# Two of the four turns of the first side group as seven block products, run side by side

## The chip, the cores and the metric

The kernel is one program on one core of a Trainium2 chip. Five engines of that core run their own instruction queues and meet only at semaphores: TensorE (PE: matrix products, weights loaded by PEld), VectorE (DVE), ScalarE (ACT), GpSimd (POOL) and SyncE (SP, which issues transfers). The metric is device time in microseconds (us) from start to end of one execution, as the median of several runs.

## The reference, cut to what matters

Two transformer-like blocks follow each other on one sequence of 256 tokens with 2048 features. All weights and results are fp32.

```
x = x + (y * silu(gate)) @ w_out                    # first block: gated MLP mixer, 3 * 4096 columns in
z = rmsnorm_2(x, g) @ w_in                          # second block, one wide product, 10256 columns
fq, fk, fv, mq, mk, mv, ...  = slices of z          # two kinds of attention heads
x = x + (g_a * (a_out @ w_proj_a) + g_m * (m_out @ w_proj_m)) @ w_out
x = x + (silu(conv(h2 @ w_up)[gate]) * conv(h2 @ w_up)[val]) @ w_down
```

Nearly all arithmetic is in such products of 256 tokens with weight matrices that are read once. The change lies in `z = ... @ w_in`: in the first 512 columns of `fq` and the first 512 of `fk`, which the kernel computes together.

## The kernel before

**A weight chunk.** The weights are one stream of chunks of 512 KB: 128 partitions by 1024 numbers, which are two blocks of 128 rows by 512 columns. Every chunk goes through the same four stations. SP loads it into one of four `raw` buffers. ACT copies it into `w_hi` in a reduced fp32 format (line 1339). DVE subtracts, `w_lo = raw - w_hi` (line 1834). PE then makes three products of each block with the activations, which are split in the same way: high with high, high with low, low with high. `w_hi` and `w_lo` have four slots each, so ACT may begin an item when PE is done with the item four places earlier.

**Items and turns.** The work is a list of items in an order that tables write out by hand. A chunk item is one chunk for both halves of the tokens: 12 matmuls of 128x512. A group is two sets of 512 columns; over 2048 rows it has four turns of 512 rows, and a turn is four chunk items (C0 to C3, C0 and C1 for the first column set, C2 and C3 for the second). A turn can also be taken as seven products of sums of blocks (the scheme of Strassen and Winograd), each an item of 6 matmuls: products 1, 5, 7, 6, 3, 2 and 4. Four blocks B11, B12, B21 and B22 of the weights are then combined: product 1 takes B11, product 5 the sum of B11 and B12, and so on. The sums of weight blocks are made by DVE (lines 1839 and 1853) and by two adding transfers that POOL issues (line 2572); the sums of the activations' rows are made once per turn ahead of time, by five DVE instructions, one ACT copy and one DVE subtraction.

**The side group.** The phase `vv` (two groups) is followed by the phase `side` (six groups). Until now the first side group has turn 0 by products and turns 1, 2 and 3 by chunks: 12 chunk items and 7 products, in the order `MID_PAIRED`. Products 1, 5, 7 and 6 go into two banks of their own (1 and 7 into one, 5 and 6 into the other); ACT copies 1, 5 and 7 out before the bank is used again, and DVE combines them (`mid_own_products`). Products 2, 3 and 4 add straight into the group's result banks.

**What else hangs on the items.** Numbered slots (`SLOTS`) tie small tasks to items; an item without a slot carries none. In slot 0, ACT and DVE split the gate weights `gw_raw` into `gw_both` (lines 1668 and 1883). In slot 2, after its item, PE makes the gate logits from `gw_both` (`gate_logits`, line 1086). The results of the first half of the group are normalised per head: ACT squares them at slot 14, DVE reduces and POOL takes a power, DVE scales them at slot 16 (`q_scaled`), and PE transposes them after slot 18 (line 833). All engines work through their queues in program order, so an instruction that waits holds everything behind it.

**SP's loads.** SP issues the ring's loads as lows are made, and the first two weight blocks of a turn by products (`mq_block`, line 681) at the items that `BLOCKS_AT` names, in the same queue.

Of the kernel before, what the change touches and what calls it, by code (L numbers as in the profile page):

```python
# [58 lines left out]
for _name, _w in (("a_norm", KD), ("norm1", KD), ("norm2", KD), ("b_s", GROUPS),  # L59
# [40 lines left out]

SUM_TURNS = {"v": (3, 2), "out1": (4, 5), "vv": (0,), "down": (0, 1, 2, 6), "gm0": (3, 2), "out2": (1,)}


SUMS_AT = {"v": (4, 8), "out1": (2, 6), "vv": (-7,), "down": (3, 7, 11, 64), "gm0": (-8, -5), "out2": (-7,)}

# [11 lines left out]

MID_TURN = 0
MID_PAIRED = ((1, "C0"), (1, "C1"), (1, "C2"), (1, "C3"), (2, "C0"), 1, 5, (2, "C1"), (2, "C2"), (2, "C3"), 7, 6,
# [9 lines left out]
NO_SLOT = {MID_PAIRED: (5, 10, 14), MID_SINGLE: (8, 14, 16), MID_EARLY: (8, 14, 16), MID_PLAIN: ()}  # L129
SLOTS = {}  # L130
# [19 lines left out]
for _name, _counts in PHASES:  # L150
    FIRST_ITEM[_name] = len(ITEMS)
    if _name == "ug":
        for _g in range(GROUPS):
            for _step in UG_ORDER if _g else UG_FIRST:
                if isinstance(_step, int):
                    ITEMS.append(Item("ug", _g, _step, UG_TURN, None, None))
                else:
                    _turn, _k = _step[0], int(_step[1][1])
                    ITEMS.append(Item("ug", _g, 0, _turn, _k // 2, 2 * _turn + _k % 2))
        continue  # L160
    if _name in MID_ORDER:
# [25 lines left out]
def in_ring(item):  # L187
# [31 lines left out]
             FIRST_ITEM["side"] - 3: ("side", B12), FIRST_ITEM["side"] - 2: ("side", B11),  # L219
             FIRST_ITEM["side"] + 64: ("side", B11, 4), FIRST_ITEM["side"] + 65: ("side", B12, 4),  # L220
             FIRST_ITEM["ug"] - 6: ("ug", B11), FIRST_ITEM["ug"] - 5: ("ug", B12),
# [38 lines left out]
def quads_ahead(phase):  # L260

    return sum(FIRST_ITEM[name] < FIRST_ITEM[phase] for name, _, _ in QUADS)


def next_in_place(item):

    if item.phase == "side" and item.group not in (0, 1):
        return None
    return (UG_NEXT_IN_PLACE if item.phase in SPREAD else NEXT_IN_PLACE).get(item.product)

# [7 lines left out]
def loads_of_block(q, b):  # L278

    return sum(phase not in SPREAD or b in (B11, B12) for phase, _, _ in QUADS[:q + 1])  # L280


def spread_quads(q):

    return sum(phase in SPREAD for phase, _, _ in QUADS[:q + 1])


def mid_quads(phase, g):

    return sum(name in MID_ORDER and (FIRST_ITEM[name], group) < (FIRST_ITEM[phase], g) for name, group, _ in QUADS)  # L290

# [14 lines left out]
def sums_made(q, p):  # L306


    ahead = sum(1 if phase == "ug" else 2 if phase in MID_ORDER else 4 for phase, _, _ in QUADS[:q])
    return ahead + ({5: 1, 4: 2} if QUADS[q][0] in MID_ORDER else {5: 1, 7: 2, 6: 3, 4: 4})[p]  # L310


def buffer_of(q, b):

    return b if b == B21 or QUADS[q][0] in SPREAD else (b + q - quads_ahead(QUADS[q][0])) % 3

# [42 lines left out]
def group_of(phase, g):  # L359
# [5 lines left out]
    else:  # L365
# [4 lines left out]
FIRST_APART_HEADS = tuple(max(0, (SLOTS["side"][_n] - HEAD_AT) // 4)  # L370
                          for _n in (MID_SINGLE.index(1) + len(MID_PAIRED), MID_SINGLE.index(1) + len(MID_PAIRED + MID_SINGLE)))

# [23 lines left out]
def build(nc, x, x_tokens, stream, w_s, params, gain_rows, final_rows, gate_w, identity, consts, out):  # L396
# [121 lines left out]
    GA_PLACE = (2, 3, 0, 1)  # L518
    mid_sums = Sums(sb, "mid", [("y", 48 * kib)], [("y", 52 * kib)], ("y", 0), ("y", 4 * kib))
    mid_wide = {}  # L520
    for name, phase, groups, blocks, halves in (
            ("mv", "vv", (0, 1), (8, 12), (40, 44)), ("mq", "side", (0,), (8, 12), (40, 44)),
            ("mk", "side", (1, 2), (56, 60), (40, 44)), ("ma", "side", (4,), (8, 12), (56, 60))):
        made = Mid(sb, name, blocks, halves, mid_sums)
        mid_wide.update({(phase, g): made for g in groups})
# [138 lines left out]
    with block:  # L664

        @block.sync
        def _(sp):
# [10 lines left out]
            def load_block(q, b):  # L678

                phase, g, _ = QUADS[q]  # L680
                sp.dma_start(wide(phase, g).blocks[buffer_of(q, b)][:], stream[block_row(q, b)]).then_inc(block_full[b], 16)


            for n, item in enumerate(ITEMS):
# [17 lines left out]
                if n in BLOCKS_AT:  # L702
# [21 lines left out]
                    load_block(QUADS.index((phase, of[0], MID_TURN)) if of else quads_ahead(phase), b)  # L724
                if n in GAIN_AT:
# [14 lines left out]
        def _(pe):  # L740
# [575 lines left out]
        def _(act):  # L1316
# [3 lines left out]
            def high_of_chunk(n):  # L1320

                item = ITEMS[n]
                if not in_ring(item):
                    b, q = PRODUCT_OF[item.product], quad_of(item)
                    of = wide(item.phase, item.group).blocks[buffer_of(q, b)]
                    if item.product in (1, 3, 2):
                        act.wait_ge(block_full[b], 16 * loads_of_block(q, b))
                    elif item.phase in SPREAD and item.product != 5 and not (item.phase in MID_ORDER and item.product == 4):
                        act.wait_ge(sem[f"block_added{item.product}"], 16 * spread_quads(q))
                    else:  # L1330
                        act.wait_ge(sem["block_sums"], sums_made(q, item.product))
# [257 lines left out]
            def mid_copies(at_item):  # L1589
# [232 lines left out]
        def _(dve):  # L1822
# [18 lines left out]
            def block_sums(n):  # L1841

                item, before = ITEMS[n], ITEMS[n - 1]
                if item.product == 1:
                    q = quad_of(item)
                    dve.wait_ge(block_full[B11], 16 * loads_of_block(q, B11))
                    dve.wait_ge(block_full[B12], 16 * loads_of_block(q, B12))
                    dve.wait_ge(lo_ready, n + 1)
                    block_sum(item, B11, B12, B11)
                elif item.phase in MID_ORDER and item.product == 2:  # L1850
                    dve.wait_ge(lo_ready, n + 1)
                    to = wide(item.phase, item.group).blocks[B11]
                    v.tensor_tensor(to[:], to[:], raw[:, CHUNK_COUNT[n] % RING, :], ALU.add).then_inc(sem["block_sums"], 1)
# [698 lines left out]
        def _(pool):  # L2552
# [6 lines left out]
            def add_block(n):  # L2559
# [10 lines left out]
                else:  # L2570
                    pool.wait_ge(lo_ready, n + 1)
                p.dma_start(wide(item.phase, item.group).blocks[to][:], stream[block_row(q, b)], accum_op=ALU.add).then_inc(
                    sem[f"block_added{product}"], 16)

# [96 lines left out]
```

## Time and profile before

| | |
|---|---|
| median of 3 runs | 2072.61 us (2071.7 to 2073.15) |
| the profiled execution, its own time | 2071.87 us |
| its span, first to last instruction | 2069.9 us |
| PE busy | 2065.7 us |
| DVE busy | 1647.2 us |
| ACT busy | 1167.7 us |

The profile is of one execution; the 1.97 us by which its own time exceeds its span lie before the first and after the last instruction. Times inside it are counted from the span's start. A busy PE is not PE at its peak: matmuls overlap, so a group's busy time per matmul is longer than the distance from one start to the next.

### The profile page before, as it was taken

The page shows a single profiled execution, that of the slowest core. Times are in us where ns is not written, and L with a number is a line of the kernel's source. Part 1 is how long each engine was busy: PE and PEld are TensorE (multiplying, and loading weights), DVE is VectorE, ACT ScalarE, POOL GpSimd, SP SyncE. Part 2 cuts the span into 40 slices and gives each one's busy share as a digit, 9 for nine tenths or more (in the row PEclk, how much of TensorE's full clock was granted, in tenths as well). Part 3 has the DMA queues.
Part 4 walks back from the last instruction along what each step waited for, and adds up shares of the span by engine and source line. Part 5 has one row for each costly group of instructions (what it writes and reads, how often), then busy time and mean ns, then how long its engine had stood idle before and what let it go on. Part 6 is the DMA issues. An engine that isn't in the chain of part 4 may idle for free.

```text
span 2069.9 us, 25490 instructions
## 1 busy us (share of the span) xinstructions
PE 2065.7 (100%) x9902; PEld 1734.3 (84%) x9902; DVE 1647.2 (80%) x1853; ACT 1167.7 (56%) x1392; POOL 50.1 (2%) x53
## 2 busy tenths in 40 slices
PE   9999999999999999999999999999999999999999
PEld 8888888888888887888888888888888888888887
DVE  7888888887888876886788778867777777789986
ACT  6766555555556555665555555555555555555553
POOL 0000000000000000110000000000000000000000
PEclk9999999999999999999999999999999999999999
DMA  9657777777684767655465656455555565556653
GB/s 345 209 198 221 224 233 226 210 245 220 247 262 153 219 206 215 206 158 192 136 232 182 206 185 219 158 187 179 190 187 191 192 196 181 193 182 236 226 202 131
DMA packets 117719, 423.28 MB, mean 204 GB/s; under 512 B 13152, under 2 KB 13920, under 8 KB 117344
## 3 DMA queue, kind: packets, MB, share of 16 engines
q1 hardware_dynamic: 109440, 394.66, 56.0%
q0 software_dynamic: 5184, 18.88, 5.2%
q10 hardware_dynamic: 2976, 8.14, 1.1%
q8 instruction: 78, 1.28, 0.2%
q14 instruction: 41, 0.34, 0.1%
HBM read 419.52 MB, written 2.10 MB: 204 GB/s over the span
## 4 chain that ended last, share of the span: by engine, by line
PE 99%; DMA 0%; ACT 0%; DVE 0%; SPq 0%; issue 0%; DVEq 0%; ACTq 0%
PE g L922 51%; PE xs L968 9%; PE xs L784 8%; PE g L784 8%; PE g L972 7%; PE g L755 4%; PE xs L790 4%; PE g L790 4%; PE xs L833 1%; PE xs L1009 1%; PE xs L1142 0%; DMA raw<-in_stream 0%; PE xs L1139 0%; PE xs L1156 0%; PE xs L1086 0%; PE xs L1169 0%
## 5 line engine op out<-in xcount | busy, mean ns | idle before, releaser
L1834 DVE TENSOR_TENSOR w_lo<-raw,w_hi 128x1024 fp32r<-128x1024 f32 x627 | 760.2, 1222 | 303.9 <-ACT w_hi L1339 296.3
L1339 ACT ACTIVATE w_hi<-raw 128x1024 fp32r<-128x1024 f32 x627 | 657.5, 1057 | 519.6 <-PE g L922 228.1
L922 PE MATMUL g<-w_hi,in_both 128*128 128x512 f32 x1104 | 350.6, 390 | 0.0
L922 PE MATMUL g<-w_hi,mid_both 128*128 128x512 f32 x960 | 310.7, 393 | 0.0
L922 PEld LDWEIGHTS g<-w_hi,in_both 128*128 128x128 f32 x1104 | 207.2, 188 | 42.9
L922 PE MATMUL g<-w_lo,in_both 128*128 128x512 f32 x552 | 214.7, 389 | 0.0
L922 PEld LDWEIGHTS g<-w_hi,mid_both 128*128 128x128 f32 x960 | 180.3, 188 | 37.3
L922 PE MATMUL g<-w_lo,mid_both 128*128 128x512 f32 x480 | 186.9, 389 | 0.0
L784 PE MATMUL g<-mlp_both,w_hi 128*128 128x512 f32 x704 | 167.0, 391 | 0.0
L784 PE MATMUL xs<-mlp_both,w_hi 128*128 128x512 f32 x704 | 165.6, 390 | 0.0
L784 PEld LDWEIGHTS xs<-mlp_both,w_hi 128*128 128x128 f32 x704 | 130.7, 188 | 26.2
L784 PEld LDWEIGHTS g<-mlp_both,w_hi 128*128 128x128 f32 x704 | 130.3, 188 | 26.0
L922 PEld LDWEIGHTS g<-w_lo,in_both 128*128 128x128 f32 x552 | 103.6, 188 | 21.3
L922 PEld LDWEIGHTS g<-w_lo,mid_both 128*128 128x128 f32 x480 | 90.3, 188 | 18.0
L922 PE MATMUL g<-w_hi,f_hi 128*128 128x512 f32 x240 | 93.5, 390 | 0.0
L922 PE MATMUL g<-w_hi,f_lo 128*128 128x512 f32 x240 | 93.4, 389 | 0.0
L922 PE MATMUL g<-w_lo,f_hi 128*128 128x512 f32 x240 | 93.4, 389 | 0.0
L790 PEld LDWEIGHTS g<-mlp_both,w_lo 128*128 128x128 f32 x704 | 88.3, 191 | 2.3
L790 PE MATMUL g<-mlp_both,w_lo 128*128 128x256 f32 x704 | 89.0, 283 | 0.0
L790 PEld LDWEIGHTS xs<-mlp_both,w_lo 128*128 128x128 f32 x704 | 87.4, 192 | 1.7
L790 PE MATMUL xs<-mlp_both,w_lo 128*128 128x256 f32 x704 | 87.9, 283 | 0.0
L1339 ACT ACTIVATE w_hi<-d_block 128x1024 fp32r<-128x1024 f32 x49 | 52.0, 1062 | 56.5 <-PE g L922 40.3
(521 smaller groups left out, 3395.7 us busy)
## 6 DMA issues: line engine op xcount, KB each, us to landing
raw<-in_stream SPq DMA_DIRECT2D x627, 512.0 KB, 4.2
d_block<-in_stream SPq DMA_DIRECT2D x28, 512.0 KB, 4.4
o_block<-in_stream SPq DMA_DIRECT2D x24, 512.0 KB, 4.8
v_block<-in_stream SPq DMA_DIRECT2D x20, 512.0 KB, 4.4
gm_block<-in_stream SPq DMA_DIRECT2D x16, 512.0 KB, 5.7
ge_block<-in_stream POOLq DMA_DIRECT2D x15, 512.0 KB, 6.0
ge_block<-in_stream SPq DMA_DIRECT2D x10, 512.0 KB, 4.9
gl_block<-in_stream POOLq DMA_DIRECT2D x6, 512.0 KB, 5.4
```

The lines of the kernel that those rows point to most:

```text
L755: ins = mm(G[buf][:, t, :], a[:, kt, at_t], w[:, slot, j * COLS:(j + 1) * COLS], start=(kt == 0 and n == 0), stop=(last and j == ROWS_PER_ ...
L784: return mm(UP[buf][:, b, :, :], w_hi[:, slot, j * COLS + b * P:j * COLS + (b + 1) * P], a_both[:, :, kt, :], start=(kt == 0), stop=last a ...
L790: ins = mm(UP[buf][:, b, 0, :], w_lo[:, slot, j * COLS + b * P:j * COLS + (b + 1) * P], a_both[:, 0, kt, :], start=False, stop=(last and j ...
L833: ins = turn(TR[:, b, t * P:(t + 1) * P], of[:, t, b * P:(b + 1) * P], ident[:])
L922: ins = mm(GG[:, bank, :], a[:, kt, t * P:(t + 1) * P], w[:, slot, half_chunk(j)], start=n == 0 and opens(item, bank), stop=ended and n == ...
L968: ins = mm(XS[:, own[p], :], a, w[:, slot, half_chunk(j)], start=first and opens_own(item), stop=last and j == 1 and n == 2, skip_group_ch ...
L972: ins = mm(GG[:, RESULT_OF[p], :], a, w[:, slot, half_chunk(j)], start=first and opens(item, RESULT_OF[p]), stop=False, skip_group_check=True)
L1009: ins = mm(SV[:, t, :], w[:, t, :], a[:, t, :], start=(n == 0), stop=(n == 2))
L1339: activation(w_hi[:, n % RING, :], of[:], ACT.Copy).then_inc(hi_ready, 1)
L1834: v.tensor_tensor(w_lo[:, n % RING, :], of, w_hi[:, n % RING, :].bitcast(F32), ALU.subtract).then_inc(lo_ready, 1)
```

## The change

The first side group now takes two turns by products, turn 0 and turn 1, and turns 2 and 3 by chunks. A table `MID_DOUBLE` writes the new order out: 8 chunk items and 14 products (a minus marks turn 1's), side by side, so that both turns' products of one number add into the same bank and are copied out once. The second turn's blocks have places of their own (`mq_block` 2 and 3), two more loads at the group's start and semaphores of their own; its row sums are made in the second `vv` group. The slots of the 22 items are again 16.

```
-SUM_TURNS = {... "vv": (0,), ...}
+SUM_TURNS = {... "vv": (0, 1), ...}
-SUMS_AT = {... "vv": (-7,), ...}
+SUMS_AT = {... "vv": (-7, 24), ...}
+MID_DOUBLE = ((2, "C0"), (2, "C1"), 1, -1, (3, "C0"), 5, -5, (3, "C1"), (2, "C2"), 7, -7, (2, "C3"), 6, -6, 2, -2, 4,
+              (3, "C2"), -4, 3, -3, (3, "C3"))
-             "side": (MID_PAIRED, MID_SINGLE, MID_SINGLE, MID_PLAIN, MID_EARLY, MID_PLAIN)}
+             "side": (MID_DOUBLE, MID_SINGLE, MID_SINGLE, MID_PLAIN, MID_EARLY, MID_PLAIN)}
+NO_SLOT = {MID_DOUBLE: (3, 6, 10, 13, 15, 19), ...}
+             FIRST_ITEM["side"] - 1: ("side", B12, 0, MID_SECOND), FIRST_ITEM["side"]: ("side", B11, 0, MID_SECOND),
-            ... ("mq", "side", (0,), (8, 12), (40, 44)),
+            ... ("mq", "side", (0,), (8, 12, 56, 60), (40, 44)),
+    def block_in(q, b):
+        return (second_full[b], 16) if second(q) else (block_full[b], 16 * loads_of_block(q, b))
...
+                if item.product == 5 and item.turn == MID_SECOND:
+                    pe.wait_ge(sem["sums_lo_ready"], sums_ahead("vv") + 2)
...
-                if p not in (1, 5, 7):
+                if p not in (1, 5, 7) or item.turn != last_by_products(phase, g):
                     return
...
+                sums_high("vv", n)
...
+                sums_low("vv", n)
+                sums_of_rows("vv", n, norm_mid.hi, norm_mid.lo)
```

On SP, where the side group's first blocks are loaded, the queue was this (`raw` are ring loads, `mq_block_113` and `mq_block_112` are B12 and B11 of turn 0):

```order
L681 DMA mq_block_113<-in_stream 128x1024
L696 DMA raw<-in_stream 128x1024 [waits lo_ready]
L681 DMA mq_block_112<-in_stream 128x1024
L696 DMA raw<-in_stream 128x1024 [waits lo_ready] x9
L681 DMA mk_block_117<-in_stream 128x1024 [waits lo_ready]
```

and is now (`mq_block_115` and `_114` are turn 0's B12 and B11, `_117` and `_116` those of turn 1):

```order
L708 DMA mq_block_115<-in_stream 128x1024
L723 DMA raw<-in_stream 128x1024 [waits lo_ready]
L708 DMA mq_block_114<-in_stream 128x1024
L723 DMA raw<-in_stream 128x1024 [waits lo_ready]
L708 DMA mq_block_117<-in_stream 128x1024
L723 DMA raw<-in_stream 128x1024 [waits lo_ready]
L708 DMA mq_block_116<-in_stream 128x1024
L723 DMA raw<-in_stream 128x1024 [waits lo_ready] x4
L708 DMA mk_block_121<-in_stream 128x1024 [waits lo_ready]
```

Two loads of 512 KB now stand between ring loads that followed each other before.

On DVE, from the last `vv` group's results (`mv_half`) to the gate weights (`gw_both`), this stood before:

```order
L2195 TENSOR_TENSOR mv_half_110<-g,mv_half_110 128x1024 [waits own_read,mm_done]
L1834 TENSOR_TENSOR w_lo<-raw,w_hi 128x1024 [waits hi_ready] x2
L2195 TENSOR_TENSOR mv_half_111<-g,mv_half_111 128x1024 [waits own_read,mm_done]
L1834 TENSOR_TENSOR w_lo<-raw,w_hi 128x1024 [waits hi_ready] x2
L2307 TENSOR_TENSOR fold<-ident 32x16
L1883 TENSOR_TENSOR gw_both<-gw_raw,gw_both 128x16x16 [waits gw_hi_ready]
```

and now:

```order
L1864 TENSOR_TENSOR w_lo<-raw,w_hi 128x1024 [waits hi_ready]
L1864 TENSOR_TENSOR w_lo<-mq_block_114,w_hi 128x1024 [waits hi_ready]
L1869 TENSOR_TENSOR mq_block_114<-mq_block_115,mq_block_114 128x1024 [waits lo_ready,block_full1,block_full0]
L2225 TENSOR_TENSOR mv_half_113<-g,mv_half_113 128x1024 [waits own_read,mm_done]
L1864 TENSOR_TENSOR w_lo<-mq_block_116,w_hi 128x1024 [waits hi_ready]
L1869 TENSOR_TENSOR mq_block_116<-mq_block_117,mq_block_116 128x1024 [waits lo_ready,second_full1,second_full0]
L1864 TENSOR_TENSOR w_lo<-raw,w_hi 128x1024 [waits hi_ready]
L2339 TENSOR_TENSOR fold<-ident 32x16
L1913 TENSOR_TENSOR gw_both<-gw_raw,gw_both 128x16x16 [waits gw_hi_ready]
```

Both block sums and the low of turn 1's product 1 now stand ahead of the gate weights on DVE.

On DVE, near the end of the group, from the small gate sums (`gr`, `b_cum`) to the first steps of combining the own products (`mq_half`), this stood before:

```order
L2323 TENSOR_SCALAR gr<-xs 128x2x8 [waits cum_ready]
L2324 COPY b_cum<-xs 128x8
L2325 COPY gr<-gz 128x2x4
L2326 TENSOR_TENSOR gr<-gz,xs 128x2x4
L1834 TENSOR_TENSOR w_lo<-raw,w_hi 128x1024 [waits hi_ready]
L1853 TENSOR_TENSOR mq_block_112<-mq_block_112,raw 128x1024 [waits lo_ready]
L1834 TENSOR_TENSOR w_lo<-raw,w_hi 128x1024 [waits hi_ready]
L2177 TENSOR_TENSOR mq_half_115<-mq_half_114,xs 128x512 [waits mm_done,p1_ready]
L1834 TENSOR_TENSOR w_lo<-mq_block_112,w_hi 128x1024 [waits hi_ready,dve_step]
```

and now:

```order
L1883 TENSOR_TENSOR mq_block_114<-mq_block_114,raw 128x1024 [waits lo_ready]
L1864 TENSOR_TENSOR w_lo<-raw,w_hi 128x1024 [waits hi_ready]
L2355 TENSOR_SCALAR gr<-xs 128x2x8 [waits cum_ready]
L2356 COPY b_cum<-xs 128x8
L2357 COPY gr<-gz 128x2x4
L2358 TENSOR_TENSOR gr<-gz,xs 128x2x4
L1883 TENSOR_TENSOR mq_block_116<-mq_block_116,raw 128x1024 [waits lo_ready]
L1864 TENSOR_TENSOR w_lo<-mq_block_114,w_hi 128x1024 [waits hi_ready]
L1864 TENSOR_TENSOR w_lo<-raw,w_hi 128x1024 [waits hi_ready]
L2207 TENSOR_TENSOR mq_half_119<-mq_half_118,xs 128x512 [waits mm_done,p1_ready]
L1864 TENSOR_TENSOR w_lo<-mq_block_116,w_hi 128x1024 [waits hi_ready,dve_step]
```

A second block sum stands in this stretch now, and the first one has moved ahead of the gate sums.

## Rows read from the trace of the kernel before

**Rows 1.** The page, parts 1 and 4: busy times, and the chain by engine.

```profile
PE 2065.7 (100%) x9902; PEld 1734.3 (84%) x9902; DVE 1647.2 (80%) x1853; ACT 1167.7 (56%) x1392; POOL 50.1 (2%) x53
...
PE 99%; DMA 0%; ACT 0%; DVE 0%; SPq 0%; issue 0%; DVEq 0%; ACTq 0%
```

**Rows 2.** Timeline, PE: start, us, engine, line, operation, idle before and its releaser.

```profile
777.49 0.39 PE L972 MATMUL g<-w_hi,mid_both 128*128 128x512 f32 x1
...
778.85 0.39 PE L972 MATMUL g<-w_hi,mid_sums_hi 128*128 128x512 f32 x1
...
794.95 0.39 PE L922 MATMUL g<-w_hi,mid_both 128*128 128x512 f32 x1
...
795.17 3.86 PE L1086 MATMUL xs<-mid_both,gw_both 128*32 128x512 f32 x16
```

**Rows 3.** Timeline, SP's issues at the group's start.

```profile
780.54 0.43 SPq L681 DMA_DIRECT2D mq_block<-in_stream  x1
782.63 29.86 SPq L696 DMA_DIRECT2D raw<-in_stream  x9
```

**Rows 4.** Tile mq_block on SP, two loads: time from issue to landing.

```profile
DMA to landing us min/median/max: 5.2/5.2/5.3
```

**Rows 5.** Windows: stretch and length, busy us of five engines, PEclk, DMA share, GB/s.

```profile
6.00:9.00 3.00, 3.00 (x15) 2.62 (x15) 2.94 (x6) 2.65 (x6) 0.00 (x0) 1.00 1.02 412
...
780.00:790.00 10.00, 10.00 (x46) 8.29 (x45) 9.49 (x10) 5.65 (x8) 0.00 (x0) 1.00 0.91 309
```

**Rows 6.** Timeline, DVE and ACT round the gate weights.

```profile
781.39 2.35 DVE L1834 TENSOR_TENSOR w_lo<-raw,w_hi 128x1024 fp32r<-128x1024 f32 x2
...
792.62 0.43 DVE L1883 TENSOR_TENSOR gw_both<-gw_raw,gw_both 128x256 fp32r<-128x256 f32 x1 [0.23 <-ACT gw_both L1668]
...
792.71 1.06 ACT L1339 ACTIVATE w_hi<-mq_block 128x1024 fp32r<-128x1024 f32 x1
...
793.80 1.23 DVE L1834 TENSOR_TENSOR w_lo<-mq_block,w_hi 128x1024 fp32r<-128x1024 f32 x1 [0.76 <-ACT w_hi L1339]
...
795.16 1.23 DVE L1839 TENSOR_TENSOR mq_block<-mq_block,mq_block 128x1024 f32<-128x1024 f32 x1
```

**Rows 7.** Timeline, DVE, ACT and PE at the end of the group and after it.

```profile
825.43 0.68 DVE L2180 TENSOR_TENSOR mq_half<-mq_half,mq_half 128x512 f32<-128x512 f32 x1
826.83 1.23 DVE L1834 TENSOR_TENSOR w_lo<-raw,w_hi 128x1024 fp32r<-128x1024 f32 x1 [0.72 <-ACT w_hi L1339]
...
829.30 2.35 DVE L1834 TENSOR_TENSOR w_lo<-raw,w_hi 128x1024 fp32r<-128x1024 f32 x2
...
840.91 1.23 DVE L2283 TENSOR_TENSOR mq_half<-mq_half,q_factor 128x1024 f32<-128x1024 f32 x1
```

**Rows 8.** Timeline, PE after the group: a small transposition, and those that want q_scaled.

```profile
828.13 0.38 PE L1110 MATMUL xs<-ident,gr 128*32 128x128 f32 x2
...
843.34 1.03 PE L833 MATMUL xs<-ident,mq_half 128*128 128x128 f32 x8
```

**Rows 9.** Timeline, ACT at an item's end: the wait that ended on PE.

```profile
779.11 1.06 ACT L1339 ACTIVATE w_hi<-raw 128x1024 fp32r<-128x1024 f32 x1 [0.30 <-PE g L972]
```

**Rows 10.** Timeline, DVE: row sums of a turn as they stand before.

```profile
687.07 1.22 DVE L1928 TENSOR_TENSOR mid_rows<-mid_both 128x1024 f32<-128x1024 f32 x1
...
689.57 0.42 DVE L1934 TENSOR_TENSOR mid_sums<-mid_rows,mid_sums 128x256 f32<-128x256 f32 x1
```

**Rows 11.** Timeline, DVE in the second vv group, where row sums are added.

```profile
763.40 1.22 DVE L1834 TENSOR_TENSOR w_lo<-mv_block,w_hi 128x1024 fp32r<-128x1024 f32 x1
765.25 1.23 DVE L1834 TENSOR_TENSOR w_lo<-mv_block,w_hi 128x1024 fp32r<-128x1024 f32 x1 [0.62 <-ACT w_hi L1339]
...
768.03 1.23 DVE L1834 TENSOR_TENSOR w_lo<-raw,w_hi 128x1024 fp32r<-128x1024 f32 x1 [0.37 <-ACT w_hi L1339]
```

**Rows 12.** Lines, DVE, 787 to 845 us: line, shape, count, busy and mean, idle before.

```profile
L1834 DVE TENSOR_TENSOR w_lo<-raw,w_hi 128x1024 fp32r<-128x1024 f32 x18 | 21.8, 1221 | 13.7 <-ACT w_hi L1339 13.7
```

**Rows 13.** Tile mq_block on POOL, two adding transfers: time from issue to landing.

```profile
DMA to landing us min/median/max: 5.4/5.6/5.8
```

More of the change, by code:

```diff
@@ L115 @@
 UG_HALF_ENDS = (16, 18)
-MID_TURN = 0
+MID_TURN, MID_SECOND = 0, 1
 MID_PAIRED = ((1, "C0"), (1, "C1"), (1, "C2"), (1, "C3"), (2, "C0"), 1, 5, (2, "C1"), (2, "C2"), (2, "C3"), 7, 6,
@@ L164 @@
                 if isinstance(_step, int):
-                    ITEMS.append(Item(_name, _g, _step, MID_TURN, None, None))
+                    ITEMS.append(Item(_name, _g, abs(_step), MID_TURN if _step > 0 else MID_SECOND, None, None))
                 else:
@@ L219 @@
              FIRST_ITEM["side"] - 3: ("side", B12), FIRST_ITEM["side"] - 2: ("side", B11),
-             FIRST_ITEM["side"] + 64: ("side", B11, 4), FIRST_ITEM["side"] + 65: ("side", B12, 4),
+             FIRST_ITEM["side"] + 67: ("side", B11, 4), FIRST_ITEM["side"] + 68: ("side", B12, 4),
+             FIRST_ITEM["side"] - 1: ("side", B12, 0, MID_SECOND), FIRST_ITEM["side"]: ("side", B11, 0, MID_SECOND),
              FIRST_ITEM["ug"] - 6: ("ug", B11), FIRST_ITEM["ug"] - 5: ("ug", B12),
@@ L268, in next_in_place @@
         return None
+    if item.phase == "side" and item.turn != last_by_products("side", item.group):
+        return None
     return (UG_NEXT_IN_PLACE if item.phase in SPREAD else NEXT_IN_PLACE).get(item.product)
@@ L278, in loads_of_block, with second @@
 def loads_of_block(q, b):
-    return sum(phase not in SPREAD or b in (B11, B12) for phase, _, _ in QUADS[:q + 1])
+    return sum(not second(k) and (QUADS[k][0] not in SPREAD or b in (B11, B12)) for k in range(q + 1))
+def second(q):
+    return QUADS[q][0] in MID_ORDER and QUADS[q][2] == MID_SECOND
 def spread_quads(q):
-    return sum(phase in SPREAD for phase, _, _ in QUADS[:q + 1])
+    return sum(QUADS[k][0] in SPREAD and not second(k) for k in range(q + 1))
 def mid_quads(phase, g):
-    return sum(name in MID_ORDER and (FIRST_ITEM[name], group) < (FIRST_ITEM[phase], g) for name, group, _ in QUADS)
+    return sum(name in MID_ORDER and (FIRST_ITEM[name], group) < (FIRST_ITEM[phase], g) for name, group in GROUPS_BY_PRODUCTS)
 def item_at_slot(phase, c):
@@ L309, in sums_made @@
     ahead = sum(1 if phase == "ug" else 2 if phase in MID_ORDER else 4 for phase, _, _ in QUADS[:q])
+    if second(q):
+        return ahead + {5: 0, 4: 2}[p]
+    if q + 1 < len(QUADS) and second(q + 1):
+        return ahead + {5: 1, 4: 3}[p]
     return ahead + ({5: 1, 4: 2} if QUADS[q][0] in MID_ORDER else {5: 1, 7: 2, 6: 3, 4: 4})[p]
 def buffer_of(q, b):
+    if second(q):
+        return b + 2
     return b if b == B21 or QUADS[q][0] in SPREAD else (b + q - quads_ahead(QUADS[q][0])) % 3
@@ L370 @@
 FIRST_APART_HEADS = tuple(max(0, (SLOTS["side"][_n] - HEAD_AT) // 4)
-                          for _n in (MID_SINGLE.index(1) + len(MID_PAIRED), MID_SINGLE.index(1) + len(MID_PAIRED + MID_SINGLE)))
+                          for _n in (MID_SINGLE.index(1) + len(MID_DOUBLE), MID_SINGLE.index(1) + len(MID_DOUBLE + MID_SINGLE)))
 def heads_before(c):
@@ L518, in build @@
     GA_PLACE = (2, 3, 0, 1)
-    mid_sums = Sums(sb, "mid", [("y", 48 * kib)], [("y", 52 * kib)], ("y", 0), ("y", 4 * kib))
+    mid_sums = Sums(sb, "mid", [("y", 48 * kib), ("y", 16 * kib)], [("y", 52 * kib), ("y", 20 * kib)], ("y", 0), ("y", 4 * kib))
     mid_wide = {}
     for name, phase, groups, blocks, halves in (
-            ("mv", "vv", (0, 1), (8, 12), (40, 44)), ("mq", "side", (0,), (8, 12), (40, 44)),
+            ("mv", "vv", (0, 1), (8, 12), (40, 44)), ("mq", "side", (0,), (8, 12, 56, 60), (40, 44)),
             ("mk", "side", (1, 2), (56, 60), (40, 44)), ("ma", "side", (4,), (8, 12), (56, 60))):
@@ L645, in build, with block_added @@
     block_full = [sem[f"block_full{b}"] for b in range(4)]
+    second_full = [sem[f"second_full{b}"] for b in (B11, B12)]
+    def block_in(q, b):
+        return (second_full[b], 16) if second(q) else (block_full[b], 16 * loads_of_block(q, b))
+    def block_added(q, product):
+        if second(q):
+            return sem[f"second_added{product}"], 16
+        return sem[f"block_added{product}"], 16 * spread_quads(q)
     hi_ready, lo_ready, mm_done = sem["hi_ready"], sem["lo_ready"], sem["mm_done"]
@@ L680, in load_block @@
                 phase, g, _ = QUADS[q]
-                sp.dma_start(wide(phase, g).blocks[buffer_of(q, b)][:], stream[block_row(q, b)]).then_inc(block_full[b], 16)
+                sp.dma_start(wide(phase, g).blocks[buffer_of(q, b)][:], stream[block_row(q, b)]).then_inc(block_in(q, b)[0], 16)
             for n, item in enumerate(ITEMS):
@@ L723, in _ @@
                         sp.wait_ge(sem["y_ready"], GROUPS)
-                    load_block(QUADS.index((phase, of[0], MID_TURN)) if of else quads_ahead(phase), b)
+                    load_block(QUADS.index((phase, of[0], of[1] if len(of) > 1 else MID_TURN)) if of else quads_ahead(phase), b)
                 if n in GAIN_AT:
@@ L1326, in high_of_chunk @@
                     if item.product in (1, 3, 2):
-                        act.wait_ge(block_full[b], 16 * loads_of_block(q, b))
+                        act.wait_ge(*block_in(q, b))
                     elif item.phase in SPREAD and item.product != 5 and not (item.phase in MID_ORDER and item.product == 4):
-                        act.wait_ge(sem[f"block_added{item.product}"], 16 * spread_quads(q))
+                        act.wait_ge(*block_added(q, item.product))
                     else:
@@ L1845, in block_sums @@
                     q = quad_of(item)
-                    dve.wait_ge(block_full[B11], 16 * loads_of_block(q, B11))
-                    dve.wait_ge(block_full[B12], 16 * loads_of_block(q, B12))
+                    dve.wait_ge(*block_in(q, B11))
+                    dve.wait_ge(*block_in(q, B12))
                     dve.wait_ge(lo_ready, n + 1)
@@ L1851, in block_sums @@
                     dve.wait_ge(lo_ready, n + 1)
-                    to = wide(item.phase, item.group).blocks[B11]
+                    to = wide(item.phase, item.group).blocks[buffer_of(quad_of(item), B11)]
                     v.tensor_tensor(to[:], to[:], raw[:, CHUNK_COUNT[n] % RING, :], ALU.add).then_inc(sem["block_sums"], 1)
@@ L2571, in add_block @@
                     pool.wait_ge(lo_ready, n + 1)
-                p.dma_start(wide(item.phase, item.group).blocks[to][:], stream[block_row(q, b)], accum_op=ALU.add).then_inc(
-                    sem[f"block_added{product}"], 16)
+                p.dma_start(wide(item.phase, item.group).blocks[buffer_of(q, to)][:], stream[block_row(q, b)], accum_op=ALU.add).then_inc(
+                    block_added(q, product)[0], 16)
             pool.wait_ge(sem["minus_half_ready"], 1)
```

8 lines of the change are left out of this document (4 added, 4 removed).

## The prediction

> **What bounds the kernel now.** I read the page first. PE is busy for 2065.7 of the 2069.9 us, and the chain that ended last runs on PE for 99% of the span [rows 1]. So only two things move the time: how much PE has to issue, and whether PE is made to wait where it does not wait now. Next I read the timeline of the first side group on PE. Six matmuls of 128x512, which are one product, start 1.36 us apart from the next six (777.49 to 778.85), so a matmul costs PE 0.227 us and a chunk item of 12 costs 2.72 us [rows 2]. The 0.39 us that stands beside each matmul overlaps with its neighbours and is not the price. Then I read the timeline of DVE and ACT there, because both must feed each item, and SP's issues and landings, because two loads are added.
>
> **The change part by part.**
>
> *Matmuls.* Turn 1 took four chunk items, 48 matmuls, and takes seven products, 42. Six matmuls fewer at 0.227 us give **-1.36 us**. This lies on the path as a whole, since PE is the path.
>
> *Row sums in the second vv group.* They add five DVE instructions, 687.07 to 689.99 in the place where they stand now, 2.9 us [rows 10], one ACT copy like the 1.06 us ones, and one DVE low of 1.2 us. They fall behind the low that ends at 763.4. The four DVE instructions that follow move by up to 2.9 us, of which the waits before them take back 0.62 and 0.37 us [rows 11], so the low at 768.03 ends near 771.2 instead of 769.3. Its item is the first chunk after product 6, and PE comes to it at 772.0: product 2 starts at 777.49 [rows 2], and two chunks of 2.72 us stand ahead of it. The cover is 0.8 us. I cost this at nothing. Were the cover gone it would cost as much as it falls short, at most 1 us, since the DVE has waits of its own again afterwards.
>
> *The gate weights: a new wait on PE.* Here I expect most of the price. Products 1 of both turns now come third and fourth in the group, where they came sixth. In the clock of the old trace PE ends the third item before the gate logits at 795.17 [rows 2]; with a product (1.36) in place of a chunk (2.72) it is ready for the gate logits at 793.81. They need `gw_both`, which DVE makes behind the low of turn 1's product 1, its block sum and the low of a chunk. That low waits for ACT, which waits for B11 of turn 1 to land, with everything else of ACT queued behind.
> - Its issue: SP issues the ring load behind the low at 781.39, at 782.63, then B12; the second low of that pair ends at 781.39 + 2.35 = 783.74, and then come another ring load and B11, at about 784.1 by my estimate [rows 3, 6].
> - Its landing: turn 0's B11 is issued at 780.54 and lands 5.2 us later, at 785.7 [rows 3, 4]. Behind it stand a ring load, B12, a ring load and B11 of turn 1, four times 0.524 MB. The fastest stretch shown moves 412 GB/s, 1.27 us each; 780 to 790 moves 309 GB/s, 1.70 us each, with a DMA share of 0.91 [rows 5]. At full share that stretch gives 340 GB/s, 1.54 us. I take 1.35 us, nearer to the faster, since the transfers then stand in line without a break: 785.7 + 5.4 = 791.1. Early end: B11 takes the same 5.2 us from its own issue, 789.3. Late end: 4 times 1.70, 792.5.
> - From there: ACT's high and the step to DVE's low take 1.09 us (792.71 to 793.80), low to block sum 1.36 us (793.80 to 795.16), the block sum and the chunk's low 1.14 each before the next may start (of two lows in 2.35 us, the first holds the second for 1.12), `fold` about 0.1 by my estimate, being far smaller than `gw_both`, and `gw_both` itself 0.43 [rows 6]. Together 5.3 us after the landing: 796.4.
> - PE is ready at 793.8, so it waits **2.6 us**; at the early end 0.8, at the late end 4.0. If the load lands before 788.5, not at all.
>
> A rule speaks here too. By the Trainium skill (DMA: Bandwidth & Descriptors, Specifications) a core's share of HBM is about 358 GB/s; that makes 1.46 us for each load as an estimate, a landing at 791.5 and a wait of 3.0 us in place of 2.6, and the sum +1.9 in place of +1.5. The trace goes above this figure for a while (412 GB/s), so the measurement decides, and the rule is no end of my range.
>
> *Lows and block sums in the group.* DVE gets three more lows and two more block sums, five times 1.22 us = 6.1 us, while PE's time for the group shrinks. From 787 to 845 us DVE stood idle for 13.7 us before lows of ring chunks alone [rows 12], so on the whole they fit; what counts is the end of the group, where eight products come close together. There DVE ran without a break from 826.83 to 842.14 (840.91 + 1.23), when `q_scaled` was done; PE asked for it at 843.34, so it was 1.2 us early [rows 7, 8]. I set both sides anew from the end of the chunk (2, C3), item 11 of the new order counted from 0:
> - DVE: its last wait is for the high of turn 1's product 2, which is item 15 and may begin when item 11 ends. From there it is 0.26 us to ACT's start (item ends at 778.85, ACT starts at 779.11) and 1.09 to DVE [rows 2, 9, 6]. Then it has the old stretch of 15.3 us, five more lows and one block sum at 1.14, two more half-size steps of 0.68 and a little for their links, and 0.3 of small gate sums, an estimate: 15.3 + 6.8 + 1.4 + 0.3 = 23.8 us [rows 7]. In all 25.2 us after item 11 ends.
> - PE: eight products and five chunks, 10.9 + 13.6, and 0.4 for a small transposition with its switch [rows 8]: 24.9 us.
> - So PE waits **0.3 us**. Bounds: none, if DVE saves as much as 0.3 us of links; 1.2 us if as much more is late as was early before.
>
> *What is hidden.* Two adding transfers more on POOL: turn 1's follow turn 0's by a block sum, and their products 7 and 6 come seven items or more later, some 14 us on PE, against landings of 5.4 to 5.8 us [rows 13]. SP's ring loads behind the added ones are delayed by two loads, about 2.7 us, against a ring that is four chunks ahead. ACT's three more highs at 1.06 us fall into its waits. Cost nothing; if one of these showed, it would be a second wait of about 1 us.
>
> **Sum**, against the profiled execution's own 2071.87 us: -1.36 + 2.6 + 0.3 = +1.5, 2073.4 us. That execution lies 0.74 us under the median of 2072.61, inside the runs' spread, so the same step from the median gives **2074.1 us**. About 0.2%, 4.1 us, is what a measurement of this kernel can tell from no change.
>
> **The rivals.**
>
> *The blocks come in time.* Then PE never waits at the gate logits, and only the saving and the 0.3 us are left: -1.1 us, 2071.5 us. For it: ring loads in the stretch are not back to back all the time, as the share of 0.91 says [rows 5]. Against it: B11 would have to land within 4.4 us of its issue, with three loads ahead of it, where turn 0's took 5.2 us with one [rows 4].
>
> *The line of loads is shared out, not served in order (slower).* Then turn 1's B11 is done with the last of its neighbours. Two more ring loads are issued at about 786 and 787, and all six behind turn 0's B11 end together, at 785.7 + 6 x 1.54 = 794.9; the gate weights are ready at 800.2, PE waits 6.4 us, and the sum is -1.36 + 6.4 + 0.3 = +5.3, 2077.9 us. This decides from a landing at about 793.7, where the sum passes +4.1. For it: nothing in the trace forbids it, since landings of 5.2 us for a load that moves in 1.3 show that loads overlap. Against it: one queue issues them all. The Trainium skill (DMA: Bandwidth & Descriptors, Queues, rings and completion order) says that each DMA engine consumes descriptors in ring order; by that rule this rival falls, and no run here shows the order yet.
>
> *DVE becomes the bound for the whole group (slower).* If none of the 6.1 us and of the 4.1 us of row sums were hidden, +10.2 - 1.4 = +8.8, 2081.4 us. Against it stand 13.7 us of waits before lows, more than these 10.2 [rows 12].
>
> **How the numbers follow.** The forecast, a wait of 0.8 to 4.0 us at the gate logits: 0.66. The blocks in time: 0.21. Shared loads: 0.09. DVE as the bound: 0.02. Anything that saves 4 us: no mechanism, since only 1.36 us is removed; 0.02. The first two lie within 0.2% of the time before: same 0.87, slower 0.11, faster 0.02. The range runs from all saved and nothing paid, -1.4, to the late end with the full 1.2 us at `q_scaled`, -1.36 + 4.0 + 1.2 = +3.8: 2071.2 to 2076.4 us. It leaves out the slower rivals alone.
>
> **What would show it.** In the timeline of PE, six matmuls fewer in the group, and a gap ahead of the sixteen gate matmuls of 1 to 4 us, where now there is none; the row of DVE's `gw_both` just before they start; ACT's high of turn 1's product 1 released by a transfer, 6 to 8 us after SP issued it. A second gap of under 1 us ahead of the transpositions of `mq_half`. No gap in `vv`. The forecast is wrong if PE waits elsewhere, or if the group's time differs from the old one's by more than the sum of these three terms.

## The result, and the profile after

The changed kernel takes 2076.44 us (median of 12 runs) where the kernel before takes 2071.69: +4.75 us, ratio 1.0022 with a 95% interval of 1.0014 to 1.0030. One run of these twelve, and one of e2's eleven below, took several times as long as the rest; the ratios leave both out, and without them the two medians fall by less than 0.1 us. The interval lies wholly above 1, but 1.002, which the prediction took as the least that can be told from no change, is inside it. The forecast was +1.5 us, 2074.1, with a range that ended at +3.8, 2076.4.

The page of the changed kernel, parts 1 and 4, to be held against [rows 1]:

```profile
PE 2065.2 (100%) x9896; PEld 1732.1 (84%) x9896; DVE 1655.7 (80%) x1864; ACT 1170.8 (56%) x1396; POOL 51.8 (2%) x55
...
PE 95%; DVE 3%; DMA 1%; issue 0%; ACT 0%; ACTq 0%; DVEq 0%; SPq 0%
```

PE has six matmuls fewer in the list, and the chain of waits now leaves PE for 5% of the span. Where it does is seen in the timeline of PE (start, us, engine, line, operation, idle before and its releaser), in the place of [rows 2]:

```profile
793.06 0.39 PE L995 MATMUL xs<-w_hi,mid_both 128*128 128x512 f32 x1
796.57 5.09 PE L1113 MATMUL xs<-mid_both,gw_both 128*32 128x512 f32 x16 [3.12 <-DVE gw_both L1913]
801.50 0.40 PE L995 MATMUL xs<-w_hi,mid_both 128*128 128x512 f32 x1
```

Two things stand here. The gate matmuls start 3.51 us after the matmul ahead of them where 0.23 is the pitch: **a wait of 3.28 us, ended by `gw_both`**. And from the first of the sixteen to what follows it takes 4.93 us (801.50 - 796.57) where 16 x 0.227 is 3.63 and the kernel before took 3.70: **1.23 us more for the same matmuls**. The windows tell why (stretch and length, busy us of five engines, PEclk, DMA share, GB/s):

```profile
786.00:793.00 7.00, 7.00 (x32) 5.80 (x31) 4.20 (x4) 3.58 (x5) 0.86 (x1) 1.00 0.99 332
793.00:796.50 3.50, 0.45 (x2) 0.02 (x1) 3.37 (x6) 3.50 (x6) 0.86 (x1) 0.91 0.48 92
796.60:799.10 2.50, 2.50 (x6) 1.02 (x7) 2.19 (x2) 0.12 (x1) 0.88 (x2) 0.50 0.98 143
799.20:801.00 1.80, 1.80 (x9) 0.87 (x8) 0.00 (x0) 0.00 (x0) 0.74 (x1) 0.98 1.02 264
```

After the wait the granted clock is 0.50, the lower of its two levels (1.2 of 2.4 GHz), where six matmuls fit into 2.5 us; then it is back at full speed. The chain of waits shows how `gw_both` came to be late (start, us, what):

```profile
782.44 1.23 DVE w_lo L1864
...
783.68 0.33 SPq L723
784.01 0.04 issue
784.06 7.21 DMA mq_block<-in_stream
791.27 0.02 issue
791.29 1.07 ACT w_hi L1368
792.36 0.02 issue
792.38 1.24 DVE w_lo L1864
...
793.74 1.23 DVE mq_block L1869
794.97 1.14 DVE w_lo L1864
796.10 0.07 DVE fold L2339
796.18 0.35 DVE gw_both L1913
796.52 0.04 issue
796.57 5.09 PE xs L1113 x16
```

This is the chain of the prediction, piece by piece: SP's ring load, turn 1's B11 issued at 784.06, 7.2 us to its landing, ACT's high, DVE's low, block sum, the chunk's low, `fold` and `gw_both`, 5.25 us from the landing to the end. At the end of the group (in the place of [rows 7, 8]) the second forecast gap stands:

```profile
845.17 1.23 DVE L2315 TENSOR_TENSOR mq_half<-mq_half,q_factor 128x1024 f32<-128x1024 f32 x1
...
846.45 0.86 PEld L860 LDWEIGHTS xs<-ident,mq_half 128*128 128x128 f32 x8 [0.54 <-DVE mq_half L2315]
```

`q_scaled` ends at 846.40 and the transpositions start at 846.45, 0.28 us late.

I summed the starts of PE's matmuls one after another over the group, against before. It is 3.69 us longer: -1.36 for six matmuls, +3.28 wait, +1.23 slow clock, +0.34 at the transpositions (0.28 and a first one slower by 0.06), +0.14 at the start of turn 1's product 3 (a low of DVE that came late), and 0.06 not placed. Outside the group the trace holds +0.24 at 873, +0.83 at 1201 and -0.53 in the start-up at 5 to 11 us, where the kernels are the same; with them the spans differ by the 4.2 us that the profiled runs show. The 0.83 contains one more wait of PE, on a part that the change leaves alone:

```profile
1202.46 0.50 PE L995 MATMUL xs<-w_hi,gm_moved_hi 128*128 128x512 f32 x1 [0.54 <-DVE w_lo L1864]
```

### The profile page after: what moved, and what is told of

Read it like the earlier page. It is cut to its first block, busy times and chain, and to the rows that moved or that the text cites. A ratio compares the mean times of both kernels' runs of the same rounds, so it can differ in the third digit from the quotient of the medians.

```text
span 2074.1 us, 25501 instructions
## 1 busy us (share of the span) xinstructions
PE 2065.2 (100%) x9896; PEld 1732.1 (84%) x9896; DVE 1655.7 (80%) x1864; ACT 1170.8 (56%) x1396; POOL 51.8 (2%) x55
## 4 chain that ended last, share of the span: by engine, by line
PE 95%; DVE 3%; DMA 1%; issue 0%; ACT 0%; ACTq 0%; DVEq 0%; SPq 0%
PE g L949 48%; PE xs L995 9%; PE xs L811 8%; PE g L811 8%; PE g L999 6%; PE g L782 4%; PE xs L817 4%; PE g L817 4%; DVE w_lo L1864 2%; PE xs L860 1%; PE xs L1036 1%; PE xs L1169 0%; DMA mq_block<-in_stream 0%; DMA gm_block<-in_stream 0%; PE g L974 0%
## 5 line engine op out<-in xcount | busy, mean ns | idle before, releaser
L949 PE MATMUL g<-w_hi,mid_both 128*128 128x512 f32 x928 | 300.5, 393 | 0.0
L949 PEld LDWEIGHTS g<-w_hi,mid_both 128*128 128x128 f32 x928 | 174.2, 188 | 36.1
L949 PE MATMUL g<-w_lo,mid_both 128*128 128x512 f32 x464 | 180.7, 389 | 0.0
```

What stands on the lines that cost most here:

```text
L949: ins = mm(GG[:, bank, :], a[:, kt, t * P:(t + 1) * P], w[:, slot, half_chunk(j)], start=n == 0 and opens(item, bank), stop=ended and n == ...
```

## The experiments

Seven kernels were run, each timed beside the kernel before (2071.78 us in the first four, 2071.61 in the last three) and profiled. Waits are those at the gate matmuls, from the timeline of PE.

| kernel | median us | ratio to before, 95% | wait | slow clock after it |
|---|---|---|---|---|
| the change | 2076.44 | 1.0022 [1.0014, 1.0030] | 3.28 | 1.23 |
| e1, once more | 2076.59 | 1.0024 [1.0014, 1.0034] | 3.57 | 1.58 |
| e2, gate weights early | 2071.12 | 0.9996 [0.9987, 1.0005] | 0 | 0 |
| e3, loads early | 2072.87 | 1.0004 [0.9995, 1.0013] | 1.25 | 0.02 |
| e4, wait filled | 2074.90 | 1.0016 [1.0007, 1.0024] | 1.63 left | 0 |
| e5, blocks change places | 2073.27 | 1.0009 [1.0000, 1.0017] | 1.51 | 0.01 |
| e6, loads late | 2078.66 | 1.0033 [1.0021, 1.0046] | 5.91 | 1.42 |
| e7, e2 and a later slot | 2070.67 | 0.9995 [0.9986, 1.0004] | 0 | 0 |

**e1, the changed kernel unaltered.**

> The changed kernel once more, unaltered, for a second trace. All theories: about 2076.4 us, PE waiting 3.0 to 3.6 us ahead of the gate matmuls, then six or seven of them 0.43 us apart and not 0.227, and 0.2 to 0.4 us ahead of the transpositions of mq_half. Two small losses of the first trace are in dispute: 0.70 us at about 1201.5 (a low of gm_block late behind its transfer) and 0.24 us at about 873. If the change brings them, by shifting the transfers, they stand in this trace again within 0.2 us; if they are chance, they are under 0.1 us or elsewhere.

Measured: 2076.59 us. The timeline of PE, and windows over the stretch behind the wait:

```profile
797.07 5.44 PE L1113 MATMUL xs<-mid_both,gw_both 128*32 128x512 f32 x16 [3.41 <-DVE gw_both L1913]
```

```profile
797.00:798.40 1.40, 1.33 (x6) 0.68 (x7) 1.40 (x3) 0.22 (x1) 0.00 (x0) 1.00 0.87 105
798.50:801.40 2.90, 2.90 (x8) 1.19 (x7) 0.78 (x1) 0.00 (x0) 1.67 (x2) 0.50 1.08 250
```

Wait and slow stretch recur. The clock falls at another moment, though: here six matmuls ran at full speed first. The losses at 873 and 1201 are not in this trace, so the change does not bring them each time. In the first trace two loads of `gm_block` took 6.9 and 6.8 us from issue to landing, in this one at most 5.9, and no later trace has the wait at 1201 again; that they landed late by chance fits this but is not shown. The wait at 873 comes back below. Summed as above, the group is 4.37 us longer than before here, against 3.69 in the first trace: the wait and the slow stretch differ from one execution to the next.

**e2, the gate weights split earlier.**

The first piece moves from ACT's loop over the side groups to that over the vv groups, the second likewise on DVE:

```
+                if c == 10:
-                if c == 0:
                     act.wait_ge(sem["gw_in"], 16)
                     activation(gw_both[:, :, 0, :], gw_raw[:].rearrange("p (a b) -> p a b", b=16), ACT.Copy).then_inc(sem["gw_hi_ready"], 1)
...
+                if c == 11:
-                if c == 0:
                     low(gw_both[:, :, 1, :], gw_raw[:].rearrange("p (a b) -> p a b", b=16), gw_both[:, :, 0, :],
                         "gw_hi_ready", 1, "gw_ready")
```

> The gate weights are split in the first vv group (slots 10 and 11), some 60 us ahead of where the changed kernel does it; all else as in the changed kernel. Theory A (gw_both is all that PE waits for there, and the slow matmuls follow from that wait): the wait of 3.3 us and the 1.2 us of slow matmuls both go, 2076.4 - 4.5 = 2071.9 us, and no gap over 0.1 us between 785 and 806. Rival B (DVE is late with everything there, so that the wait only moves to the next items): the lows of turn 1's product 1 and of the chunk behind it end at 793.6 and 796.1 in the first trace, PE would want them at about 797 and 798; by B half or more of the 3.3 us comes back before them, 2073.5 to 2075 us.

Measured: 2071.12 us, 5.3 under the change and not told apart from before. The timeline of PE:

```profile
793.54 0.39 PE L995 MATMUL xs<-w_hi,mid_both 128*128 128x512 f32 x1
793.76 3.86 PE L1113 MATMUL xs<-mid_both,gw_both 128*32 128x512 f32 x16
```

No wait, no slow matmul, and none comes back behind them: theory A. B11 landed no sooner (792.76, ACT's high at 792.79); PE spends 3.7 us on the gate matmuls while DVE catches up. So the loads that the change adds cost PE nothing by themselves. They cost because one thing that PE wants early stood behind them on DVE.

**e3, the loads earlier; e5, the loads in the other order.**

In e3, and below it in e5:

```
-FIRST_ITEM["side"] - 1: ("side", B12, 0, MID_SECOND), FIRST_ITEM["side"]: ("side", B11, 0, MID_SECOND),
+FIRST_ITEM["side"] + (-8): ("side", B12, 0, MID_SECOND), FIRST_ITEM["side"] + (-7): ("side", B11, 0, MID_SECOND),
```

```
-FIRST_ITEM["side"] - 1: ("side", B12, 0, MID_SECOND), FIRST_ITEM["side"]: ("side", B11, 0, MID_SECOND),
+FIRST_ITEM["side"] + (0): ("side", B12, 0, MID_SECOND), FIRST_ITEM["side"] + (-1): ("side", B11, 0, MID_SECOND),
```

> Turn 1's B12 and B11 are loaded 7 items earlier (with the 8th and 7th item ahead of the group, in place of the last and the first of the group); all else as in the changed kernel. Theory A (the landing of B11 at 791.3 is the head of the chain that ends in gw_both): B11 lands before 785.6, ACT's high of turn 1's product 1 follows that of turn 0 at about 787, DVE goes on without that wait, and gw_both is ready at 793 to 794.5 where PE wants it at 793.3: a wait of 0 to 1.2 us, and the matmuls behind it at 0.227, so 2071.9 to 2073.1 us. Rival C (DVE's row sums and block sums, not the load, make gw_both late): the wait stays at 2.5 us or more, 2075.5 us or more.

> Turn 1's two blocks change places in the line: B11 is loaded with the last item ahead of the group and B12 with the first of the group; all else as in the changed kernel. Theory A (the chain from B11's landing): B11 lands where B12 did, at 788.4 to 788.9; ACT's high follows at once, DVE's low of turn 1's product 1 then stands behind a mv_half step until 790.4, its block sum needs B12, which lands at 791.3, and gw_both is ready at about 794.4 where PE wants it at 793.3: a wait of 1.1 us, no slow matmuls if a wait like the 1.2 and 1.6 us of the two kernels run before leaves the clock alone, 2076.5 - 2.2 - 1.3 = 2073.0 us. Rival F (only the last of the two loads counts): gw_both stays at 796, 2076.5 us.

Measured: 2072.87 and 2073.27 us, waits of 1.25 and 1.51. Timeline of DVE in e3:

```profile
789.59 1.22 DVE L2225 TENSOR_TENSOR mv_half<-g,mv_half 128x1024 f32<-128x1024 f32 x1
790.72 1.21 DVE L1864 TENSOR_TENSOR w_lo<-mq_block,w_hi 128x1024 fp32r<-128x1024 f32 x1
792.07 1.23 DVE L1869 TENSOR_TENSOR mq_block<-mq_block,mq_block 128x1024 f32<-128x1024 f32 x1
793.21 1.22 DVE L1864 TENSOR_TENSOR w_lo<-raw,w_hi 128x1024 fp32r<-128x1024 f32 x1
794.35 0.15 DVE L2339 TENSOR_TENSOR fold<-ident 32x16 f32<-32x16 f32 x1
794.43 0.41 DVE L1913 TENSOR_TENSOR gw_both<-gw_raw,gw_both 128x256 fp32r<-128x256 f32 x1
```

The blocks had landed by 775.6, and DVE now works through without an idle row; what is left of the wait is its own work. So the landing is worth 3.28 - 1.25 = 2.0 us of the wait, and DVE's row of work the other 1.25: A for the larger part, C for the smaller. In e5 B11 landed at 789.0 instead of 791.3, which took 1.8 us off the wait; the wait of 1.5 us was 0.4 over what I expected, as DVE's `mv_half` step ran until 791.1.

**e4, PE kept at work while it waits.**

```
+    for k in range(13):
+        mm(OUT[0:32, :], norm_mid.hi[:, 0, 0:32], norm_mid.both[:, :, 0, :], start=True, stop=True)
     pe.wait_ge(sem["gw_ready"], 1)
```

PE's wait for the place of the results (`own_read`) moves ahead of these matmuls.

> Thirteen matmuls more (32 x 512 results that the gate matmuls overwrite, so nothing computed changes) are put ahead of PE's wait for gw_both, 13 x 0.227 = 2.95 us of work in a wait of 3.28; all else as in the changed kernel. Theory D (the matmuls behind the wait are slow because PE stood still): all sixteen gate matmuls 0.227 apart, PEclk 1.00 in that stretch, 2076.4 - 1.2 = 2075.2 us, though PE has more to do. Rival E (they are slow for a reason of their own, as what runs beside them): unchanged, 2076.4 us, with the same six or seven 0.43 us apart.

Measured: 2074.90 us, 1.5 to 1.7 us faster than the two medians of the changed kernel, with thirteen matmuls more. The intervals of the ratios overlap, but nine of its eleven runs are faster than every run of the changed kernel, e1 included. The timeline of PE, and windows over the wait that is left and the gate matmuls:

```profile
795.48 3.17 PE L1112 MATMUL xs<-mid_both 128*32 128x512 f32 x13
800.12 3.86 PE L1115 MATMUL xs<-mid_both,gw_both 128*32 128x512 f32 x16 [1.47 <-DVE gw_both L1915]
```

```profile
798.40:800.10 1.70, 0.25 (x2) 0.00 (x0) 1.70 (x5) 1.70 (x2) 0.86 (x1) 1.00 0.00 0
800.20:803.00 2.80, 2.80 (x13) 1.35 (x14) 2.13 (x2) 0.08 (x1) 1.23 (x2) 1.00 1.02 152
```

The wait left was longer than planned, since B11 landed later in this execution, but the clock stays at 1.00 and the gate matmuls take 3.70 us: theory D. This trace also holds two waits of 1.4 and 0.5 us at 52 and 57 us, far from any edit, which the other traces lack; the profiled execution took 2077.63 us, the slowest of the eleven, so the median is the better figure.

**e6, the loads later.**

```
-FIRST_ITEM["side"] - 1: ("side", B12, 0, MID_SECOND), FIRST_ITEM["side"]: ("side", B11, 0, MID_SECOND),
+FIRST_ITEM["side"] + (1): ("side", B12, 0, MID_SECOND), FIRST_ITEM["side"] + (2): ("side", B11, 0, MID_SECOND),
```

> Turn 1's B12 and B11 are loaded one item later each, so that one more ring load stands ahead of B11 in the line; all else as in the changed kernel. In order (each load ends as the next begins to land, 1.1 to 1.5 us apart): B11 lands 1.1 to 1.5 us later than at 791.3, PE waits 4.4 to 5.1 us, the slow matmuls cost 1.2 to 1.6 us as before, 2077.6 to 2078.2 us. Shared out (a load takes 7.2 us or more from its own issue, which is 2.6 us later): a wait of 5.9 us or more, 2079 us or more.

Measured: 2078.66 us and a wait of 5.91, past what serving in order was to give. The chain of waits, windows, and the DMA queues from 792 to 794 (queue, packets, MB, share of 16 engines; q1 carries SP's loads, q0 POOL's adding transfers):

```profile
786.95 7.11 DMA mq_block<-in_stream
794.05 0.02 issue
794.08 1.06 ACT w_hi L1368
```

```profile
790.00:792.00 2.00, 2.00 (x10) 1.65 (x10) 0.97 (x1) 0.00 (x0) 0.86 (x1) 1.00 1.00 340
792.00:794.00 2.00, 1.60 (x8) 0.98 (x6) 0.00 (x0) 0.00 (x0) 0.00 (x0) 1.00 0.88 166
```

```profile
q0 software_dynamic: 65, 0.27, 79.9%
q1 hardware_dynamic: 22, 0.07, 8.1%
```

The size is that of the shared line, the landings are not: the three loads that SP issued at 786.10, 786.47 and 786.95 landed at 790.77, 792.86 and 794.05, in order, none together. What held the last two back is not settled. POOL's adding transfer was issued at 790.13, and the rate falls to 166 GB/s, but the queues show whose rate that is: from 792 on it is mostly the adding transfer's own, while all that is left of SP's loads is 22 packets, 0.07 MB, at 8.1% of the engines, which is about one engine's work. In the packets of the trace SP's 4 KB pieces take 0.16 us each, at the end as before, and a row of eleven follows without a gap from 792.06 to 793.78. So the adding transfer is not seen to slow them. The rows read as if B11 landed late because one or two of the 16 engines still had their share of it to move. Why these were behind stays open, and no run took the adding transfer away. The wait follows the landing one for one: B11 lands 2.63 us later than in the changed kernel (2.78, less 0.15 by which the two start-ups differ), and the wait is 2.63 us longer.

**e7, e2 with the transpositions a slot later.**

The edits of e2, and:

```
-QK_T_AT = (18, 20, 34, 37, 50, 53)
+QK_T_AT = (19, 20, 34, 37, 50, 53)
```

> The gate weights split in the first vv group as in e2, and PE's first transpositions of mq_half one slot later (19 for 18). Theory G (the wait of 0.29 us ahead of them is q_scaled, late behind DVE's other work, and there is a slot of slack behind it): that wait goes, 0.3 us under e2's 2071.1, about 2070.8 us. Rival H (what follows from those transpositions is as tight, so the wait moves to the next ones or to the first scores): 2071.1 us or more, with a gap of 0.3 us or more at another place between 843 and 870.

Measured: 2070.67 us. The gap ahead of the transpositions is gone, and PE is 0.4 us further at 860. The timeline of PE at the next tight place, and of ACT and DVE ahead of it:

```profile
862.97 1.06 ACT L1368 ACTIVATE w_hi<-mk_block 128x1024 fp32r<-128x1024 f32 x1 [3.02 <-DMA mk_block<-in_stream]
...
867.32 1.23 DVE L1867 TENSOR_TENSOR w_lo<-raw,w_hi 128x1024 fp32r<-128x1024 f32 x1 [0.20 <-ACT w_hi L1368]
...
868.86 0.47 PE L995 MATMUL xs<-w_hi,mid_sums_hi 128*128 128x512 f32 x1
```

PE needs a low that ends at 868.55, behind ACT's high of `mk_block`, which an adding transfer held until 862.95. In e2 the same matmul stands at 868.87, so the 0.4 us gained at the transpositions was nearly all given back here (0.36): rival H by the trace. This is also the place of the changed kernel's 0.24 at 873. The median is 0.45 us under e2's, less than the spread of runs. Of the versions that were run e7 is the fastest, by 5.8 us against the change; against before it is 0.9 us ahead, which the interval of 0.9986 to 1.0004 does not settle.

## Why the prediction was right in its mechanism and short in its size

- *Matmuls, -1.36 us:* right. Over the group alone e2 is 0.85 us shorter than before, which is -1.36 with the 0.34 and 0.14 of the group's end and 0.03 not placed.
- *Row sums in vv, put at nothing:* right for `vv` itself. The low that was to end near 771.2 in the old clock started at 769.32 and ended at 770.55, in a trace that runs 0.53 us ahead, and PE has no wait in vv. But DVE had not caught up when the side group's loads were issued. Before, it had 0.79 us to spare ahead of the low that lets SP go on (first line); now it comes to that low without a pause (second line), in the old clock 0.44 us later, and SP issues turn 0's B11 as much later, at 780.46 (third line; in the old clock 780.99, before 780.54). That the row sums are what DVE had not caught up with is read from these rows; no run took them away:

```profile
778.92 1.23 DVE L1834 TENSOR_TENSOR w_lo<-raw,w_hi 128x1024 fp32r<-128x1024 f32 x1 [0.79 <-ACT w_hi L1339]
...
778.83 1.23 DVE L1864 TENSOR_TENSOR w_lo<-raw,w_hi 128x1024 fp32r<-128x1024 f32 x1
...
780.46 0.43 SPq L708 DMA_DIRECT2D mq_block<-in_stream  x1
```

- *The wait at the gate weights, 2.6 us:* right in place, releaser and chain, mis-sized by 0.7. PE was ready at 793.29, which is the forecast 793.8 less the 0.53 of the start-up; from landing to `gw_both` 5.25 us passed against 5.3. The load was late: 791.27, in the old clock 791.8 and not 791.1. Two terms were too small. "I take 1.35 us" for each load in line is the lesser: the four loads behind turn 0's B11 (785.56 to 791.27) took 1.43 each, 5.7 us against 5.4. The other 0.4 us is the start of that line, 785.7, which was taken over from the trace before: turn 0's B11 was issued 0.45 us later, behind the row sums, and took its 5.1 us from there.
- *A wait costs its length:* this unspoken step is the largest single part of the miss. The clock fell to its lower level in the wait or soon behind it, and the gate matmuls took 1.23 us more (1.58 in e1, 1.42 in e6); e4 shows that PE's standing still is the cause. With the 1.23 us the forecast would have been 2.7 us above before, still below 0.2%. The Trainium skill (TensorE: Matmul & The Clock Gate, What's actually happening) says that the clock is granted by how busy PE has been recently, and is 1.2 GHz when it is idle, 2.4 when it is busy. The three traces agree, with 0.427 us a matmul in place of 0.227.
- *The group's end, 0.3 us:* right for the transpositions (0.28) and by its own path: from the end of item 11 at 821.27 DVE took 25.1 us and PE 24.9, as reckoned. But DVE's lateness also cost 0.14 us at turn 1's product 3 and 0.06 in the first transposition, so 0.5 in all.
- *What is hidden:* POOL's adding transfers took 5.9 to 8.7 us in the first trace, up to 11.6 in e2, and not the 5.4 to 5.8 of [rows 13], and still no product of the group waited for one. In the next group PE lost 0.24 us in the first trace and 0.36 in e7 behind an adding transfer, which I had not looked for.
- *The rivals:* "the blocks come in time" fell, as the chain shows. "Shared out, not in order" fell by the landings: in each of these traces SP's loads round the group land in the order of issue, in the full line 1.1 to 1.9 us apart, once 2.1 (e6). The Trainium skill (DMA: Bandwidth & Descriptors, Queues, rings and completion order) says that each DMA engine consumes descriptors in ring order, though not that transfers complete in that order. These landings agree. "DVE as the bound for the whole group" fell: in e2 PE waits for nothing between 785 and 829.

The corrected sum, -1.36 + 3.28 + 1.23 + 0.54 = +3.7, is the group as the first trace has it. The prediction's own last test, that the group's time differs by no more than its three terms (+1.5), therefore fails. The medians say +4.75 and +4.8. Of the 1 us beyond +3.7, e1 shows that up to 0.7 can lie in the group, where it is 4.37 us longer; the rest I cannot place firmly: waits of 0.2 to 1.4 us on late transfers come and go between traces of like kernels. The step of +4.75 is also above the end of the range, +3.8. That 2076.44 us nevertheless stands at the range's upper end of 2076.4 is luck: the three runs before, from which the range was set, had a median 0.92 us above that of the twelve.

## What to carry to other kernels

When loads are added ahead of a wait, look for everything that stands behind the waiting step on the same engine; here a small split of gate weights, which could have been done 60 us earlier, stood behind three steps of DVE that began with a wait for a load, and cost 4.5 us. Move such a step out of the line before pricing the loads: that alone gave back all that the change lost (e2). Follow work that is hidden where it stands to the next transfers that wait for the same engine: the row sums cost nothing in `vv`, and some 0.4 us at the head of the next line of loads. And price an idle stretch of PE by the clock behind it as well as by its length: waits of 1.25 to 1.63 us cost themselves, those of 3.3 to 5.9 us cost 1.2 to 1.6 us more.

## What the runs showed of the hardware that I had not expected

- The clock may fall after PE has taken up work again: in e1 six matmuls behind the wait ran at full speed before 2.9 us at 0.50. Work put into the wait, though useless, made the program 1.5 us faster (e4).
- An adding transfer of POOL moves its bytes at a fraction of the rate that plain loads have at the same share of the engines. In the changed kernel one or two of them alone moved 143 GB/s at a DMA share of 0.98 (796.6 to 799.1, behind the wait), SP's plain loads alone 383 GB/s at the same share, and both together 264 GB/s at 1.02 (799.2 to 801):

```profile
786.00:791.00 5.00, 5.00 (x23) 4.13 (x22) 3.58 (x3) 1.87 (x3) 0.86 (x1) 1.00 0.98 383
```
